# Moving sixteen modulation units of layer 2 from the feed-forward of layer 1 into its mixer

## What is computed

```python
mod_x = sc @ w_ada[i] + b_ada[i]                      # 1 x 6144, from the condition c alone
mod_c = scc @ w_ada[i] + b_ada[i]
sh1, sc1, ga1, sh2, sc2, ga2 = jnp.split(mod_x, 6)
hx = rms_norm(x, g_mix[i]) * (1.0 + sc1) + sh1
zx = hx @ w_in[i]
mx = concat(latent_attention(q, k, v, kc, vc), pool_mix(...), fourier_mix(...))
x = x + ga1 * (mx @ w_out[i])
fx = rms_norm(x, g_ffn[i]) * (1.0 + sc2) + sh2
x = x + ga2 * swiglu(fx, w_gate_up[i], w_down[i])
```

## Time and profile before

| | us |
|---|---|
| median of 3 executions | 2386.36 |
| lowest, highest | 2386.0, 2391.59 |
| profiled execution, time | 2390.24 |
| profiled execution, span | 2388.1 |
| TensorE busy in the span | 2322.0 |
| VectorE busy | 1304.7 |
| ScalarE busy | 1068.5 |

### The profile page before, as it was taken

One profiled execution on the slowest core, in us unless ns is written; L12 is line 12 of the kernel. 1 busy time (PEld: TensorE's weight loads), 2 busy tenths in 40 slices (PEclk: granted clock), 3 DMA queues, 4 the chain that ended last, 5 costly groups with the idle time before them and its releaser, 6 DMA issues.

```text
span 2388.1 us, 37602 instructions
## 1 busy us (share of the span) xinstructions
PE 2322.0 (97%) x15018; PEld 1940.3 (81%) x15018; DVE 1304.7 (55%) x2293; ACT 1068.5 (45%) x2046; POOL 33.7 (1%) x40
## 2 busy tenths in 40 slices
PE   8999999999889999999999999999999999999999
PEld 6658877878858999777667788888888887799999
DVE  5454433333645556567886434534434778756665
ACT  4343422222545455545556423522323765655443
POOL 0300000000100000000000000000000000000000
PEclk9999999999999999999999999999999999999999
DMA  8473333333265555255554322222222222154554
GB/s 311 168 272 109 99 113 124 117 129 105 101 234 178 190 178 182 89 190 190 196 201 160 106 97 83 86 97 97 97 97 97 84 94 71 59 165 145 190 183 144
DMA packets 95324, 336.06 MB, mean 141 GB/s; under 512 B 10672, under 2 KB 12720, under 8 KB 95024
## 3 DMA queue, kind: packets, MB, share of 16 engines
q1 hardware_dynamic: 95152, 333.67, 40.9%
HBM read 332.58 MB, written 1.05 MB: 140 GB/s over the span
## 4 chain that ended last, share of the span: by engine, by line
PE 85%; DVE 6%; ACT 5%; issue 2%; DMA 2%; SPq 0%; ACTq 0%; DVEq 0%
PE out L1420 23%; PE out L1422 23%; PE out L1421 23%; PE sc L1493 2%; DMA raw<-stream 2%; DVE w_lo L1816 2%; PE pt L1502 1%; PE out L1371 1%; PE pv L1520 1%; ACT w_hi L1559 1%; PE pt L1371 1%; PE pv L1518 1%; PE aux L1331 1%; DVE stage L2135 1%; ACT e_t L1709 1%
## 5 line engine op out<-in xcount | busy, mean ns | idle before, releaser
L1420 PE MATMUL out<-act_hi,w_lo 128*128 128x512 f32 (+1 forms) x2144 | 742.8, 346 | 10.6 <-DVE w_lo L1816 4.6
L1421 PE MATMUL out<-act_lo,w_hi 128*128 128x512 f32 (+1 forms) x2144 | 729.5, 340 | 0.0
L1422 PE MATMUL out<-act_hi,w_hi 128*128 128x512 f32 (+1 forms) x2144 | 729.2, 340 | 0.0
L1559 ACT CAST w_hi<-raw 128x1024 fp32r<-128x1024 f32 (+2 forms) x444 | 452.5, 1022 | 426.0 <-PE out L1422 418.2
L1816 DVE TENSOR_TENSOR w_lo<-raw,w_hi 128x1024 fp32r<-128x1024 f32 (+2 forms) x444 | 528.5, 1193 | 127.0 <-ACT w_hi L1559 126.8
L1420 PEld LDWEIGHTS out<-act_hi,w_lo 128*128 128x128 f32 x2144 | 408.6, 191 | 67.2 <-issue 15.0
L1422 PEld LDWEIGHTS out<-act_hi,w_hi 128*128 128x128 f32 x2144 | 408.3, 190 | 45.2
L1421 PEld LDWEIGHTS out<-act_lo,w_hi 128*128 128x128 f32 x2144 | 408.7, 191 | 42.9
L1420 PE MATMUL out<-mix_hi,w_lo 128*128 128x256 f32 (+1 forms) x1186 | 389.7, 329 | 3.3 <-DVE mix_lo L1838 1.5
L1421 PE MATMUL out<-mix_lo,w_hi 128*128 128x256 f32 (+1 forms) x1186 | 388.0, 327 | 0.0
L1422 PE MATMUL out<-mix_hi,w_hi 128*128 128x256 f32 (+1 forms) x1186 | 387.9, 327 | 0.0
(11 more groups left out here) (254 smaller groups left out, 2340.5 us busy)
## 6 DMA issues: line engine op xcount, KB each, us to landing
raw<-stream SPq DMA_DIRECT2D x604, 512.0 KB, 3.6
raw<-stream SPq DMA_DIRECT2D x16, 384.0 KB, 3.3
raw<-stream SPq DMA_DIRECT2D x16, 256.0 KB, 2.6
x<-xin SPq DMA_DIRECT2D x4, 512.0 KB, 5.7
consts<-const SPq DMA_DIRECT2D x1, 1344.0 KB, 7.6
x<-ctx SPq DMA_DIRECT2D x1, 1024.0 KB, 5.7
out<-x SPq DMA_DIRECT2D x8, 128.0 KB, 1.7
consts<-const SPq DMA_DIRECT2D x1, 320.0 KB, 5.4
```

Source lines behind the costliest of these rows:

```text
L1420: nc.tensor.matmul(ps, wl, xh, start=(k == 0), stop=False)
L1421: nc.tensor.matmul(ps, wh, xl, start=False, stop=False)
L1422: ins = nc.tensor.matmul(ps, wh, xh, start=False, stop=(k == s.nk - 1))
L1559: nc.scalar.copy(w_hi[:, number % HL, 0:n], raw[:, place[number] % RAW, 0:n]).then_inc(S["hi_ready"], 1)
```

## The change

The second bank of layer 2 goes into the list of the mixer of layer 1, and the feed-forward gets an empty list. The mixer then has 64 units. An item takes five, three at its first pump and two at its second. Four more pumps of one unit each are put into the list of other work.

```diff
-        if not both:
-            for at in (9, 8, 7, 6, 2, 1):
-                work.insert(at, lambda: pump(1))
+        for at in (10, 9, 2, 1) if both else (9, 8, 7, 6, 2, 1):
+            work.insert(at, lambda: pump(1))
         per = -(-len(work) // 4)
...
-    seam = layer_first(0, ada_list(0, [1, 2]) + ada_list(1, [0]), 4, r)
-    seam = ffn(0, NT, [lambda a=a: ada(*a) for a in ada_list(1, [1])], seam)
+    seam = layer_first(0, ada_list(0, [1, 2]) + ada_list(1, [0, 1]), 5, r)
+    seam = ffn(0, NT, [], seam)
```

## The result

The changed kernel took 2393.89 us in the median of 20 executions (2389.05 to 2397.4), the kernel before 2390.01 us (20 executions, 2385.87 to 2395.47). The ratio is 1.0017, with a 95% interval of 1.0011 to 1.0022: slower by 4.1 us, 2.6 to 5.3. The forecast was slower by 5.3 us and inside what can be told. One execution in the last experiment, of 4564.65 us, was in a slow state and is left out of its ratio. The profiled execution has a span of 2393.5 us, against 2388.1.

A forecast was written before the change was run, and what follows sets the result against it. TensorE, busy for 97% of the span, was taken to bound the kernel. The terms -12.0 + 7.2 + 10.8 - 0.7 = +5.3 us on the median 2386.4 gave 2391.7, rounded to 2391.5 us, range 2381 to 2401.

The forecast's parts named there:

- The feed-forward: Feed-forward of layer 1: sixteen units taken out of a full TensorE queue give back 0.75 us each, -12.0 us.
- The units in the mixer: Mixer of layer 1: sixteen more units at 0.43 us and three more groups at 0.12 cost TensorE +7.2 us.
- the sum: Whole kernel: -12.0 + 7.2 + 10.8 - 0.7 = +5.3 us, put on the median 2386.4, rounded to 2391.5 us.
- The waits for loads: Mixer of layer 1: TensorE's waits for unit loads grow from 1.3 to 12.1 us, +10.8 us.
- The rule of the turnaround: Ring of four: an entry is usable no sooner than about 5.3 us after the entry four places ahead.
- The smaller terms: Mixer items: waits for VectorE and ScalarE are covered by load waits, -0.7 us; mixer end even, other places 0.
- The exchange at the end: Mixer end: the 0.99 us low-part wait is covered, but w_out waits about 1.0 us for the transpose; even.
- The loads keep up: Rival, mixer: loads land near 3.1 us, waits total 3 to 5 us, time 2383; chance 0.20.
- The clock falls as well: Rival, mixer: waits make the granted clock fall, one fall +8 us, two +10.7, time 2397.5; chance 0.24.
- All is hidden: Rival, mixer: waits stay at 1.3 us, units fill 1.5 us of idle time, -6.3 us, 2379.5 with luck; chance 0.06.
- the signs: Changed profile: feed-forward 12.0 us shorter, 512 unit records, 1 to 2 us waits, w_out at 204, DMA above 300 GB/s.

The follow-up runs named there:

- the last experiment: The changed kernel without the four single pumps between dependent steps, so nine units are left for the mixer's end: 2399.7 us, ratio 1.0035 to the kernel before.
- The pair without waits: Changed kernel and kernel before, each with a quarter of the bytes loaded for layer 1's mixer units: 2383.3 us (ratio 0.9967) and 2387.21 us (0.9987).

## Why the prediction was right

**The feed-forward, -12.0 us.** Measured -12.4, and 0.76 us a unit where fourteen were left out.

**The units in the mixer, +7.2.** One, two, three and four units take 0.55, 0.97, 1.41 and 1.84 us to the next operation where none waits, as the sum had them. The pair without waits grows by 6.6, and this has the smaller terms in it.

**The waits for loads, +10.8.** In the changed kernel the groups of units last 12.3 us longer, from start to start and less the transpose at the end, than groups of their size do without a wait. In front of two groups the first unit waits as well, 0.8 us in item 0 and 0.2 in item 9, and 0.35 us in item 8 are the clock. That makes 13.0; before it was 1.3. So +11.7 against +10.8. The sum is better than its parts. By item, forecast and measured: item 0 1.5 and 1.65, item 1 0.1 and 1.3, item 2 1.45 and 0.5, item 3 0.95 and 0.55, item 4 1.95 and 1.3, item 5 0 and 0.5, item 7 0.1 and 0.2, item 8 1.45 and 2.45, item 9 0.35 and 1.0, item 10 2.0 and 0.9, item 11 1.95 and 1.4, the end 0.3 and 1.2. The rule of the turnaround finds the places where waits can be (only items 1 and 5 are missing, 1.8 us together). It does not find their size, since a single load took anything from 3.3 to 7.1 us. That the sum comes so near is in part luck: items 2, 3, 4, 10 and 11 were forecast 3.7 us too high together, all others and the end 4.5 too low. The median of 4.6 that the sum used was too low by 0.4; the loads come more densely now, at 272 GB/s over the mixer instead of 254.

That the waits come from the number of places, and not from the mean rate of the DMA engines, was argued from one ratio and is shown by the runs with five places. It holds with a limit: in items 9 to 11 the average binds as well, which the run with three pumps brought out and the prediction only hinted at.

**The smaller terms.** In the items -0.7 did not come: TensorE waits 0.68 us for ScalarE's copy in front of a Fourier step, where before it waited 0.41 and 0.33 for VectorE and ScalarE. But in front of the last PV it waits 0.33 instead of 0.72, and with the Fourier block right behind the query sums a step of the queries takes 0.3 us less to the next. From start to start the smaller terms come to -0.9, near the forecast for other reasons. The exchange at the end was right: 0.89 us for the transpose in place of 0.99.

**The rivals.** *The loads keep up* fell with the first number, 5.0 us to landing. The estimate of 3.2 us from the Trainium skill (DMA: Bandwidth & Descriptors, Anatomy of one DMA) agrees here with the least landing alone (3.3); for a quarter of the bytes, where the same rule gives an estimate of 2.3 us, the median is 2.5, and for half of them, estimate 2.6, it is 3.2. The page states its rule for loads that GpSimd issues; here SyncE issues them, with up to four in flight. *The clock falls as well* came true in small: one dip of 3.41 us, in item 8, behind the longest wait, about 1.6 us. By its own sign, a granted clock below 1.00 in the mixer, the prediction was wrong in the clock. *All is hidden* needed a rate of 333 GB/s without waits; the mixer reached 272, and 317 from item 8 on.

**The sum.** In the mixer 19.6 us against 17.3: 0.9 more of waits, the dip of 1.6, and 0.2 less in the smaller terms. -12.4 + 19.6 is +7.2, and the first unit of the mixer starts 0.84 us later already, for reasons ahead of the change: 8.1 us at 621. The profiled execution ends only 5.4 us later. 2.7 us were given back in layers 2 to 4, which the change does not touch. Waits that both traces have show where: the changed kernel is 8.1 us behind at 613.12, 7.0 at 680.46, 7.4 at 1863.45 and 5.4 at 2112.49 (times of the kernel before; of the changed one 621.21, 687.49, 1870.83 and 2117.89). The last 2 us go with the clock. Between the last two, the kernel before has it at 0.50 in two stretches, the changed one only from 2083.0 to 2089.9. Of the kernel before:

```profile
2075.90:2079.30 3.40, 3.40 (x16) 3.12 (x16) 2.02 (x7) 2.93 (x6) 0.00 (x0) 0.50 0.47 154
2092.95:2099.78 6.83, 5.98 (x28) 5.98 (x29) 5.13 (x9) 3.78 (x5) 0.00 (x0) 0.50 0.56 161
```

Not every such stretch costs time. Of the kernel before, too:

```profile
1854.02:1860.85 6.83, 6.83 (x34) 6.74 (x33) 3.87 (x11) 5.31 (x15) 0.00 (x0) 0.50 0.15 57
```

The changed kernel has 1.00 there, but behind it TensorE waits 0.96 us for VectorE (at 1870.83) instead of 0.19 (at 1863.45), and it has not caught up. From two profiled executions it cannot be said how much of the 2.7 us is due to the change. The ratio of the twenty says 4.1 in all.

**The time and the signs.** The sum was put on the median of three executions, 2386.36; twenty have 2390.01. So the time of 2391.5 came within 2.4 us of the 2393.89 measured by a base that was 3.7 too low and a difference that was 1.3 too high; that they cancel is chance. Of the signs, w_out at 204 (206.83), the feed-forward shorter by 12.0 (12.4), and 512 records (512) came, the first 2.8 us late. The waits of 1 to 2 us in items 2, 4, 8, 10 and 11 came in two of them, 4 and 11; the others had 0.5, 2.45 and 0.9. DMA above 300 GB/s over the mixer did not come, with 272; the prediction's own bytes over its own time, 34.3 MB in about 120 us, give 286.

## What to carry to other kernels

When loads go through a ring of buffers, compare the time from one use to the use as many places later as the ring has with the turnaround (here 0.67 us to the issue and some 5 to the landing), for the order in which they are really used: with four places, two and two an item waited for 1.3 us in the whole mixer, three and two for 13. Work that fills idle time must find both the engine and its loads idle; moving work out of a full queue saved its full price here (0.76 us a unit) and was paid for with 7 us for the units themselves and 12 more of waits for loads. One more place in the ring was worth more (10 us without the move) than any order of the units that was tried.

## What the runs showed that was not expected

In the mixer of the changed kernel a load of 512 KB took 5.0 us in the median with four places in use, 5.6 with five, 3.2 at half its size and 2.5 at a quarter. It is not the places alone: in the kernel before, with fewer units, it was 4.6 with four and 4.3 with five. Halving the size took 1.8 us off; at 349 GB/s, which the short items reached with five places, half of the bytes are only 0.75 us (0.262 MB / 349 GB/s). The rest is likely time behind other loads; no run separates it. The granted clock fell to half behind stretches of 6.83 us with TensorE busy for 4.50, 4.79 and 4.18 us of them (once, at the head of the mixer, for 5.76), and the one of 4.18, in front of w_out, cost more (3.8 us) than the waits that led to it (2.4).
